# Moving 32 single-element gathers from the head of an up pass into its queries' stretch

## The reference, cut to what matters

```python
def peer_ffn(h, wq, subkeys, u_tab, v_tab):          # 128 tokens at a time
    q = (hb @ wq).reshape(128, 8, 2, 128)             # the queries
    s = einsum('thpd,hpnd->thpn', q, subkeys)         # scores against 2 x 128 subkeys per head
    ...                                               # top 16 of 16384 experts per head -> idx, g
    a = gelu(einsum('td,thkd->thk', hb, u_tab[idx]))  # one activation per token and chosen expert
    return einsum('thk,thkd->td', g * a, v_tab[idx])  # weighted sum of 128 expert rows per token
```

## Time and profile before

| what | value |
|---|---|
| median of 3 runs | 4878.59 us (4877.94 to 4879.81) |
| the profiled execution, span | 5238.6 us |
| PE busy in it | 4681.2 us, 89% |
| DVE busy | 3122.9 us, 60% |
| POOL busy | 1844.4 us, 35% |
| ACT busy | 1521.2 us, 29% |

### The profile page before, as it was taken

The page is one execution under the profiler, slowest core; times in us unless marked ns, Lnnn a source line. Parts: engine busy times, 40 slices in busy tenths (PEclk is TensorE's granted clock), DMA queues, the critical chain, the costliest instruction groups (busy, mean ns, idle before and its releaser), DMA issues.

```text
span 5238.6 us, 75656 instructions
## 1 busy us (share of the span) xinstructions
PE 4681.2 (89%) x25798; PEld 3894.8 (74%) x25798; DVE 3122.9 (60%) x6247; ACT 1521.2 (29%) x2757; POOL 1844.4 (35%) x1918
## 2 busy tenths in 40 slices
PE   8889899999878886898889988799999988999998
PEld 6569789999777775555555556588899977778886
DVE  2673646666356666545555564746575775666777
ACT  2332423534212124000000022435254454222222
POOL 1111210000455657666666530113000035666652
PEclk9999999999889989999999998899999999999999
DMA  4331115756478972888999972211365743889997
GB/s 152 113 105 55 31 71 185 224 174 211 149 245 297 307 269 76 316 315 322 326 325 331 351 272 70 98 63 41 133 201 168 226 144 122 324 314 337 347 351 266
DMA packets 316699, 1103.74 MB, mean 211 GB/s; under 512 B 59392, under 2 KB 108672, under 8 KB 267872
## 3 DMA queue, kind: packets, MB, share of 16 engines
q1 hardware_dynamic: 165024, 648.09, 36.0%
q0 software_dynamic: 151488, 453.35, 24.3%
HBM read 1037.13 MB, written 62.03 MB: 210 GB/s over the span
## 4 chain that ended last, share of the span: by engine, by line
PE 68%; issue 9%; another core or an unknown queue 7%; DVE 7%; POOL 4%; ACT 4%; DMA 1%; POOLq 1%; ACTq 0%; DVEq 0%; PEldq 0%; SPq 0%
PE PS L1280 17%; PE PS L1355 14%; PE PS L1364 7%; PE PS L1379 6%; PE PS L1225 5%; PE PS L1262 3%; PE PS L938 3%; PE PS L936 3%; POOL arena L671 3%; PE PS L1179 3%; PE PS L1018 2%; PE PS L997 1%; PE PS L1075 1%; DVE PS L2492 1%
## 5 line engine op out<-in xcount | busy, mean ns | idle before, releaser
L1280 PE MATMUL PS<-hS,wS 128*128 128x256 f32 x7680 | 978.3, 290 | 79.0 <-ACT wS L1687 49.7
L1355 PE MATMUL PS<-hS,ring 128*128 128x256 f32 x4096 | 969.5, 387 | 79.6 <-issue 70.0
L671 POOL DMA_INDIRECT arena<-hx,arena x768 | 810.8, 1056 | 631.6 <-POOLq L406 333.1
L1280 PEld LDWEIGHTS PS<-hS,wS 128*128 128x128 f32 x7680 | 958.1, 197 | 96.6 <-issue 84.7
L1355 PEld LDWEIGHTS PS<-hS,ring 128*128 128x128 f32 x4096 | 791.6, 194 | 269.8 <-issue 154.6
L2522 DVE TENSOR_TENSOR wS<-ring,wS 128x1024 fp32r<-128x1024 f32 x320 | 391.9, 1225 | 465.6 <-ACT wS L1687 370.6
L677 POOL DMA_INDIRECT arena<-in_experts,arena x465 | 476.7, 1025 | 530.3 <-DVE PS L2492 394.3
L2492 DVE SCALAR_TENSOR_TENSOR PS<-arena,PS 128x1024 f32<-128x1024 f32 x462 | 593.2, 1284 | 25.9 <-DMA arena<-in_experts,arena 9.0
L1364 PE MATMUL PS<-ring,arena 128*128 128x512 f32 x1024 | 483.3, 616 | 35.1 <-DVE arena L2659 29.3
L1805 ACT ACTIVATE arena<-PS 128x256 f32<-128x256 f32 x256 | 97.1, 382 | 1301.5 <-PE PS L1355 710.6
L2659 DVE TENSOR_TENSOR arena<-arena 128x256 f32<-128x256 f32 x256 | 109.4, 427 | 565.4 <-ACT arena L1805 424.2
(11 more groups left out here) (332 smaller groups left out, 6284.3 us busy)
## 6 DMA issues: line engine op xcount, KB each, us to landing
ring<-in_experts SPq DMA_DIRECT2D x256, 1024.0 KB
ring<-in_experts SPq DMA_DIRECT2D x384, 512.0 KB
ring<-in_wcat SPq DMA_DIRECT2D x80, 1024.0 KB
hx<-arena SPq DMA_DIRECT2D x384, 128.0 KB
ring<-in_wq SPq DMA_DIRECT2D x40, 1024.0 KB
arena<-in_rpb POOLq DMA_DIRECT2D x96, 128.0 KB, 2.6
arena<-hx,arena POOLq DMA_INDIRECT x768
arena<-xs POOLq DMA_DIRECT2D x20, 512.0 KB, 5.2
```

The source lines that it names most:

```text
L671: pool.indirect_dma_start(out=aX[n][:, k:k + 1], out_offset=None, in_=src, in_offset=bass.IndirectOffsetOnAxis(ap=at[:, k:k + 1], axis=0)) ...
L1280: mm = pe.matmul(bank[6 + c % 2][:, 0:PASS], u[:, k, :], hS[:, h, k, :], start=(part == 0 and k == 0), stop=(part == 2 and k == KD - 1))
L1355: mm = pe.matmul(bank[c % 2][:, 0:PASS], u[:, k, :], hS[:, 0, k, :].bitcast(F32), start=(k == 0), stop=(k == KD - 1))
```

## The change

The 32 single gathers ahead of the wait for the normed tokens are dropped from there, and each half tile of the queries is followed by four single gathers in place of two. The number of gathers, their order and all their data are the same; nothing else is touched.

```diff
                         rows0 = t.get("rows", 0)
-                        take_activations(3, f0, range(32))
                         pool.wait_ge(s["xn_ready"], t["normed"])
                         for n in range(16):
                             pool.wait_ge(s["pq_done"], 16 * t["pass"] + n + 1)
-                            take_activations(3, f0, range(32 + 2 * n, 34 + 2 * n))
+                            take_activations(3, f0, range(4 * n, 4 * n + 4))
                         pool.wait_ge(s["s_done"], 8 * (t["pass"] + 1))
```

## The result

The changed kernel takes 4902.21 us (median of 7 runs, 4894.76 to 4907.95) against 4882.90 us for the kernel before (7 runs, 4877.94 to 4889.43). The ratio is 1.0039, with a 95% interval of 1.0029 to 1.0048, so it is slower by 0.29% to 0.48%, or 14 to 23 us. The forecast was 4900.1 us, or 21.5 us more; the middle of the measured interval is 19 us.

A forecast was written before the change was run, and what follows sets the result against it. PE was taken to bound the pass whenever it is fed. 18.1 us (late first row gather) + 1.4 (stretched gathers) + 2.0 (PE's clock) = 21.5 us on 4878.6, giving 4900.1 us; 8-in-10 range 4885 to 4906.

The forecast's parts named there:

- The holes of the first profile are that execution's own: PE's pauses in the 5238.6 us profiled execution of the kernel before: claimed absent from timed runs, which keep a 6.32 us beat.
- the count: Time lost against PE's undisturbed beat wherever gathers run: 366 us in sum, against 360.0 us of profiled excess over the median.
- the four stretches: Head and rest of the second up pass, dense stages of layers 0 and 1: 30.2, 119.9, 166.6 and 49 us lost.
- The head gives nothing back: Start of the second up pass: dropping 32 single gathers gains 0, out of a possible 0 to 30.2 us.
- First row gather 18.1 us late, and 1.4 more from gathers beside DVE's low parts: POOL in the queries: four gathers need 5.0 us per 3.9 us half tile; two stretched gathers add 1.4 us.
- No slack at step 20, so PE's pause is 19.5 us: Second up pass: PE asks for the low part at 1474.6, ready at 1475.6, so 19.5 us of row lateness stops PE.
- The clock costs 2.0 us: PE after the pause in step 20: matmuls run slower for a while, taken as 2.0 us.
- Nothing is given back: Rest of the pass after step 20: POOL keeps up, PE has no idle time, so 0 us is recovered.
- the hole in the head: Rival: the 32-gather burst really costs PE 30.2 us at the pass's start; the change gives 4869.9 us; chance 0.09.
- its twin in the queries' stretch: Rival: 64 gathers in a burst cost PE up to 60 us during the queries, 4930 us; chance 0.05.
- quicker gathers without the profiler: Rival: POOL's pace in timed runs is under 1.09 us a gather, so the change does little, about 4884 us; chance 0.12.
- a late row: Likeliest case: POOL's backlog in the queries delays row 0 and PE waits in step 20; 4900 us, chance 0.74.

The follow-up runs named there:

- the second profile: The kernel before with no edit, run and profiled once more: 4881.73 us, profiled span 4880.1 us.

## Why the prediction was right, step by step

- *The holes of the first profile are that execution's own.* Right, and shown by the second profile. The lengths worked out for undisturbed dense stages, 873.9 and 788 us, measured 874.1 and 787.4. The head and the rest of the pass were put too short, at 52.3 and 354.8 us; they take 57.5 and 365.8. So it is in part luck that the count came within 6 us of the 360. It took in 16 us that an undisturbed execution loses as well, and about 8 us of the real excess lay in none of the four stretches. I had called the holes the mark of a profiled execution; the later profiles don't have them, so it was the one execution and not profiling.
- *The head gives nothing back.* Right: 57.5 us with the gathers and 57.7 without.
- *First row gather 18.1 us late, and 1.4 more from gathers beside DVE's low parts.* Right. It was issued 86.3 us behind the start of the queries in place of 66.3, 20.0 us late against 19.5 forecast. The two stretched gathers took 1.77 and 1.74 us, 1.6 more than two plain ones. Here the Trainium skill ("SBUF — State Buffer", "Who interferes with whom") infers that a tensor_tensor leaves descriptor generation alone; a gather stretched beside each of the two low parts speaks against that, for these gathers at least. The same section has a tensor_tensor with both inputs in SBUF contend with GpSimd's reads, and each gather takes its row numbers from a tile in SBUF. No run here tells whether it was that read or the making of the descriptors that waited.
- *No slack at step 20, so PE's pause is 19.5 us.* This term was 1.7 us too large: the pause was 17.76. The issue was 0.5 us later than forecast, and two parts go the other way. Row 0 reached DVE 5.9 us behind its issue in the second profile of the kernel before and 4.3 us behind it in the changed one, so it was 18.4 us late at DVE and not 20.0; why it landed sooner stays open. And there was a slack of about 0.8 us, where I had found none: undisturbed, row 1 is taken at 1440.85 and the low part is done at 1443.26, where PE asks at about 1444.1. The low part was 18.6 us late in the changed kernel, and 17.76 of that became the pause. I had read the slack from a disturbed profile, in which row 1 was taken 1.9 us later, counted from the start of the queries. The 1475.6 for the low part was worked out and not read there; it ran at 1479.98, because ACT's high part of that step stood behind a hole:

```profile
1478.62 0.38 ACT L1695 ACTIVATE arena<-PS 128x256 f32<-128x256 f32 x1 [12.03 <-remote]
1478.90 1.05 ACT L1687 ACTIVATE wS<-ring 128x1024 fp32r<-128x1024 f32 x1
...
1479.98 1.23 DVE L2522 TENSOR_TENSOR wS<-ring,wS 128x1024 fp32r<-128x1024 f32 x1 [5.64 <-issue]
```

- *The clock costs 2.0 us.* Right in size. Behind the pause 8 matmuls took 2.08 us in place of 1.22 behind a short pause, and the plain step took 4.72 in place of 3.61: 2.0 together, with a granted clock of 0.50 over those 8 matmuls. The same 2.08 stands behind a pause of 9.27 and of 37.88 us.
- *Nothing is given back.* Nearly right. 17.76 + 2.0 = 19.8, and L grew by 18.2. The other 1.6 are a difference of small pauses: behind the queries PE loses about 11 us to them in the kernel before, which I had put at none, and about 9 in the changed one. My reading that POOL keeps up beside the rows (2.51 us a row against 2.67) was too kind. The stretched gathers add 0.22 us a row, and POOL issued a row every 2.73 us, a little over what DVE's program asks; DVE waited 54 times for rows.

The rivals: the hole in the head fell with the second profile, its twin in the queries' stretch fell with the 61.97 us that this stretch takes in both kernels, and quicker gathers without the profiler fell with the timed runs, which moved by 19 us. A cost that sets in between three and four gathers a half tile, and 20 us more for the next 16 gathers, are what a late row predicts and a cost per gather doesn't.

## What to carry to other kernels

A queue that is idle early and full later should have its movable work in the early gap, even if nobody needs the results yet. When work is moved into a stretch, compare the queue's time per beat with the beat: under it the move is nearly free (-4 to +6 us here for 16 gathers), above it the backlog lands on whatever stands behind it on that queue, here the first row gather and through DVE's program order a matmul. And a profile whose span is far from the timed median should be reconciled with it, stretch by stretch, before any of its holes is taken for a cost.

## What the runs showed that I had not expected

One profiled execution of an unchanged kernel was 358 us longer than the next (5238.6 against 4880.1 us), with about 350 us of the excess in the four stretches counted in the prediction. All four have gathers beside PE's work, but the queries' stretch, with two gathers a half tile, had no excess (61.98 us against 61.97). What set it off stays open. And relieving POOL by 24 gathers beside the rows brought nothing by itself (-4 to +4 us), four rows of lead alone brought 3 us at best guess, and the two together 6. That the two need each other is a guess from these three figures and the waits: their intervals overlap, and it wasn't tested further.
